# Gate units 5 and 6 of layer 0 as three-pass products, changed orders in layer 0, and blank products at the inner norms

## The reference, cut to what matters

```
z = x @ w_in                        # 1024 -> q 512, k 128, v 128, u 512, two gates of 1024
a = sliding_window_attention(q, k, v, sinks, rel_bias)
s = s5_mixer(u, ...)                # complex diagonal scan, gelu, y * sigmoid(y @ w_glu + b)
merged = sigmoid(g_attn) * (a @ w_branch_attn) + sigmoid(g_ssm) * (s @ w_branch_ssm)
x = layer_norm(ALPHA * x + merged @ w_out)
ffn = swiglu(x) in layer 0, top-2-of-8 experts in layer 1
ple = sigmoid(x @ w_gate) * (p @ w_proj)
x = layer_norm(ALPHA * x + ffn + ple)
```

## Time and profile before

| | us |
|---|---|
| median of three timed runs | 1611.16 |
| the profiled execution's own time | 1609.16 |
| its span in the profile | 1607.3 |
| PE busy | 1570.6 |
| VectorE busy | 1354.6 |
| ScalarE busy | 999.9 |
| PE waiting for VectorE at the norms' transposes (line 1048) | 6.2 + 1.3 |
| PE waiting for the load of a unit of w_in | 2.4 |
| PE waiting for ScalarE before turn_values | 2.1 |

### The profile page before, as it was taken

The page is one execution under the profiler, slowest core; times in us unless marked ns, Lnnn a source line. Parts: engine busy times, 40 slices in busy tenths (PEclk is TensorE's granted clock), DMA queues, the critical chain, the costliest instruction groups (busy, mean ns, idle before and its releaser), DMA issues.

```text
span 1607.3 us, 24068 instructions
## 1 busy us (share of the span) xinstructions
PE 1570.6 (98%) x9028; PEld 1332.7 (83%) x9028; DVE 1354.6 (84%) x1300; ACT 999.9 (62%) x913; POOL 149.8 (9%) x157
## 2 busy tenths in 40 slices
PE   8999999999999999999999999999999999999996
PEld 6889799999899978888888888888888888888884
DVE  8797856655687788999998999998999998999998
ACT  7345444334546437776777777777677677767763
POOL 2000139940300000000000000000000000000000
PEclk9999999999999999999999999999999999999998
DMA  7535855554444568999999999999999999999993
GB/s 225 162 107 183 301 180 192 185 183 132 130 132 148 200 230 297 360 372 359 361 369 334 351 369 370 352 366 334 351 371 360 354 377 332 345 377 364 360 361 124
DMA packets 169448, 456.55 MB, mean 284 GB/s; under 512 B 7638, under 2 KB 60919, under 8 KB 168872
## 3 DMA queue, kind: packets, MB, share of 16 engines
q1 hardware_dynamic: 168472, 450.87, 78.1%
q0 software_dynamic: 768, 4.75, 0.8%
q10 hardware_dynamic: 144, 0.05, 0.0%
HBM read 453.02 MB, written 2.62 MB: 283 GB/s over the span
## 4 chain that ended last, share of the span: by engine, by line
PE 86%; DVE 8%; issue 3%; DMA 1%; ACT 1%; SPq 0%; DVEq 0%; ACTq 0%
PE psum L735 20%; PE psum L737 20%; PE psum L736 20%; PE psum L742 6%; PE psum L744 6%; PE psum L743 6%; PE psum L845 4%; DVE wl L466 2%; PE psum L1199 1%; PE psum L871 1%; ACT wh L460 1%; PE psum L802 1%; DMA ring<-in_w_pg 1%; DVE hid L2190 1%; DMA ring<-in_w_in 1%
## 5 line engine op out<-in xcount | busy, mean ns | idle before, releaser
L466 DVE TENSOR_TENSOR wl<-ring,wh 128x2048 fp32r<-128x2048 f32 x269 | 609.3, 2287 | 67.0 <-ACT wh L460 63.2
L460 ACT ACTIVATE wh<-ring 128x2048 fp32r<-128x2048 f32 x307 | 581.7, 1920 | 126.3 <-PE psum L737 78.4
L736 PE MATMUL psum<-wl,xgh 128*128 128x512 f32 x896 | 349.2, 390 | 0.0
L735 PE MATMUL psum<-wh,xgh 128*128 128x512 f32 x704 | 282.0, 401 | 1.0 <-DVE xgl L2174 0.5
L737 PE MATMUL psum<-wh,xgl 128*128 128x512 f32 x704 | 274.9, 390 | 0.0
L736 PEld LDWEIGHTS psum<-wl,xgh 128*128 128x128 f32 x896 | 168.5, 188 | 32.4
L735 PE MATMUL psum<-wh,hidh 128*128 128x512 f32 x440 | 172.7, 393 | 3.7 <-DVE wl L466 2.8
L736 PE MATMUL psum<-wl,hidh 128*128 128x512 f32 x448 | 174.4, 389 | 0.0
L737 PE MATMUL psum<-wh,hidl 128*128 128x512 f32 x440 | 171.4, 390 | 0.0
L466 DVE TENSOR_TENSOR wl<-ring,wh_spare 128x2048 fp32r<-128x2048 f32 x72 | 164.5, 2284 | 3.0 <-ACT wh_spare L460 3.0
L735 PEld LDWEIGHTS psum<-wh,xgh 128*128 128x128 f32 x704 | 132.2, 188 | 33.6 <-DVE wl L466 5.5
(11 more groups left out here) (435 smaller groups left out, 2769.5 us busy)
## 6 DMA issues: line engine op xcount, KB each, us to landing
ring<-in_moe_gu SPq DMA_DIRECT2D x224, 1024.0 KB, 7.2
ring<-in_moe_dn SPq DMA_DIRECT2D x112, 1024.0 KB, 7.3
ring<-in_w_in SPq DMA_DIRECT2D x25, 1024.0 KB, 5.4
ring<-in_w_gu SPq DMA_DIRECT2D x22, 1024.0 KB, 5.1
ring<-in_w_dn SPq DMA_DIRECT2D x11, 1024.0 KB, 4.9
ring<-in_w_out SPq DMA_DIRECT2D x8, 1024.0 KB, 6.2
ring<-in_w_pg SPq DMA_DIRECT2D x8, 1024.0 KB, 5.2
ring<-in_w_ba SPq DMA_DIRECT2D x4, 1024.0 KB, 5.1
```

The lines of the kernel that those rows point to most:

```text
L460: eng.activation(parts(u)[0], ring[:, ring_slot(u), :], ACT.Copy).then_inc(hi_ready, 1)
L466: eng.tensor_tensor(lo, ring[:, ring_slot(u), :], hi.bitcast(F32), ALU.subtract).then_inc(lo_ready, 1)
L735: pe.matmul(dst, ah, bh, start=first, stop=False, skip_group_check=True)
L736: pe.matmul(dst, ah, bl, start=False, stop=False, skip_group_check=True)
```

## The change

Five things.
1. PLAIN names the plain units of layer 0: 0 to 4, 7 and 8. Units 5 and 6 become split, with high parts in ring slots 4 and 5, and `split_index` counts accordingly. ScalarE writes x0h after the copy of unit 2's q, then the high part of unit 5; that of unit 6 follows copy_maps. VectorE makes both remainders between xIl and scan_states(0).
2. SP issues the load of the state maps of layer 0 (`raw`) after the load of unit 1 instead of before it.
3. local_products(0) stands before turn_values on PE, and ScalarE copies v before k (in both layers).
4. In layer 0 unit 15's high part, and the remainders of 14 and 15, move to the places that they have in layer 1.
5. `turn` begins with `stay_awake`: after `var_ready` of the block PE does AWAKE = 3 plain products of 256 columns with constants into the bank that it turns the block into next. Their results are overwritten.

```
--- before.py
+++ after.py
@@ -42,8 +42,8 @@
 FSTEPS = DFF // 256
 ESTEPS = DFE // 512
 MIXER_UNITS = 22
-FIRST_SPLIT = 9
-PLAIN_UNITS = FIRST_SPLIT
+PLAIN = (0, 1, 2, 3, 4, 7, 8)
+PLAIN_UNITS = len(PLAIN)
 MIXER_RING = 4
 RING_ORDER = (2, 3, 0, 5, 1, 4)
 FREED_BY = {22: 18, 23: 19, 24: 20, 25: 20, 26: 21, 27: 21}
@@ -59,9 +59,11 @@
 LATE_HI = {12: "ring4", 13: "ring5", 14: "late", 15: "ring4", 16: "ring5", 17: "norm", 18: "ring4", 19: "late", 20: "ring5", 21: "ring4"}
 EARLY_HI = {i: ("ring4", "ring5", "early")[i % 3] for i in range(11)} | {11: "turns"}
 ROUNDS = ((0, range(8)), (1, range(4)), (1, range(4, 8)))
-HI_PLACE = ({i: p for i, p in (EARLY_HI | LATE_HI).items() if i >= FIRST_SPLIT}, EARLY_HI | LATE_HI)
+GATE_HI = {5: "ring4", 6: "ring5", 9: "ring4", 10: "ring5", 11: "turns"}
+HI_PLACE = (GATE_HI | LATE_HI, EARLY_HI | LATE_HI)
 EARLY = 4
 WARM = 6
+AWAKE = 3
 GELU_C = 0.7978845608028654
 BIAS_W = 3 * P
 
@@ -394,11 +396,11 @@
 
         def is_split(l, i):
 
-            return l == 1 or i >= FIRST_SPLIT
+            return l == 1 or i not in PLAIN
 
         def split_index(u):
 
-            return u - PLAIN_UNITS
+            return u - sum(p < u for p in PLAIN) if isinstance(u, int) else u - PLAIN_UNITS
 
         def split_used(eng, u, laps=0):
 
@@ -649,10 +651,10 @@
                         load(u, src, ring_slot(u))
                     u += 1
                     if u == 1:
-                        sp.dma_start(raw.rearrange("p a b c -> p (a b c)"), bc_in[0]).then_inc(raw_dma, 16)
                         sp.dma_start(relb_sb[0:BUCKETS + 1], relb).then_inc(table_dma, 16)
                         sp.dma_start(hot_sb[0:BUCKETS + 1], hot_in).then_inc(table_dma, 16)
                     if u == 2:
+                        sp.dma_start(raw.rearrange("p a b c -> p (a b c)"), bc_in[0]).then_inc(raw_dma, 16)
                         small_loads()
                     if u == RING:
                         skew_bias()
@@ -940,7 +942,7 @@
                     project("q")
                     turn_maps(0)
                     project("kv")
-                    turn_values(), local_products(0), input_states(0), scores(0)
+                    local_products(0), turn_values(), input_states(0), scores(0)
                     project("g")
                     input_states(1)
                 else:
@@ -1039,8 +1041,15 @@
                     mm.then_inc(unit_used, 1)
                 u += 4
 
+                def stay_awake(n, b, times):
+
+                    pe.wait_ge(var_ready, NB * n + b + 1)
+                    for _ in range(times):
+                        pe.matmul(bank[OUT_BANKS[2 * b]][:, 0:SEQ], ident, cst[:, 0:SEQ], start=True, stop=True)
+
                 def turn(src, b):
 
+                    stay_awake(1 if src is xa else 2 * l, b, AWAKE)
                     pe.wait_ge(ln_ready, b + 1 + (NB if src is xa else 2 * NB * l))
                     for q in range(2):
                         ps = bank[OUT_BANKS[2 * b + q]]
@@ -1389,15 +1398,18 @@
                     act.activation(qT[:, 2 * (g - 2):2 * (g - 1), :], src, ACT.Copy, scale=HD ** -0.5).then_inc(qk_ready, 1)
                     act.wait_ge(qk_ready, 4 * l + g - 1)
                     act.nop().then_inc(g_free[g % 2], 1)
-                    early_hi(3 + g)
+                    if l:
+                        early_hi(3 + g)
+                    elif g == 2:
+                        act.activation(x0h[:], xT[:], ACT.Copy).then_inc(x0_hi, 1)
+                        early_hi(5)
                 if l == 0:
-                    copy_maps(0)
-                    act.activation(x0h[:], xT[:], ACT.Copy).then_inc(x0_hi, 1)
+                    copy_maps(0), early_hi(6)
+                act.activation(vt.rearrange("p a b -> p (a b)"), group(4)[:, 1, :], ACT.Copy).then_inc(v_ready, 1)
                 for kv in range(2):
                     for q in (0, HD):
                         ins = act.activation(kT[q:q + HD, kv, :], group(4)[kv * HD:(kv + 1) * HD, 0, :], ACT.Copy)
                 ins.then_inc(qk_ready, 1)
-                act.activation(vt.rearrange("p a b -> p (a b)"), group(4)[:, 1, :], ACT.Copy).then_inc(v_ready, 1)
                 act.wait_ge(qk_ready, 4 * l + 3)
                 act.wait_ge(v_ready, l + 1)
                 act.nop().then_inc(g_free[0], 1)
@@ -1439,13 +1451,10 @@
                     if m % 2:
                         act.wait_ge(glu_th, 4 * l + m + 1)
                         act.nop().then_inc(g_free[g % 2], 1)
-                if l == 1:
-                    early_hi(15)
+                early_hi(15)
                 for b in range(2):
                     act.wait_ge(s_ready, 2 * l + b + 1)
                     act.activation(gsh[:, 2 * b:2 * b + 2, :], sT[:, 2 * b:2 * b + 2, :], ACT.Copy, scale=0.25).then_inc(s_hi, 1)
-                if l == 0:
-                    early_hi(15)
                 gates(), copy_probs(2), early_hi(16), copy_attended(2), early_hi(17)
                 for k in range(KD):
                     act.wait_ge(m_ready, KD * l + k + 1)
@@ -2002,6 +2011,7 @@
                     output_powers(dve, link, 0, (scratch_a[:, 0:512], scratch_b[:, 0:512]), 8, (0,))
                     dve.wait_ge(x0_hi, 1)
                     dve.tensor_tensor(xIl[:], xT[:], x0h[:].bitcast(F32), ALU.subtract).then_inc(x0_lo, 1)
+                    early_lo(5), early_lo(6)
                     scan_states(0), logits(0)
                     normalise(0), scan_states(1)
                     output_powers(dve, link, 0, temps, 8, (8,))
@@ -2014,14 +2024,9 @@
                 gelu_half(1), early_lo(12)
                 dve.wait_ge(gelu_ready, 2 * (l + 1))
                 gelu_lo(0), gelu_lo(1), attended_lo(1), logits(2), early_lo(13), normalise(2)
-                if l == 1:
-                    early_lo(14), gated(0), gated(1), early_lo(15)
-                else:
-                    gated(0), gated(1), early_lo(14)
+                early_lo(14), gated(0), gated(1), early_lo(15)
                 dve.wait_ge(s_ready, 2 * (l + 1))
                 gated_lo(0), gated_lo(1)
-                if l == 0:
-                    early_lo(15)
                 attended_lo(2), early_lo(16)
 
 
```

## The result

| us | before | after |
|---|---|---|
| median of five runs each | 1610.77 (1608.92 to 1612.85) | 1603.73 (1603.16 to 1604.67) |
| the profiled execution | 1609.16 | 1603.33 |
| its span | 1607.3 | 1601.5 |
| its mean granted clock | 0.995 | 0.997 |

The ratio of the medians is 0.9948, 95% interval [0.9934, 0.9961]: the change makes the kernel 7.0 us faster. The forecast was 1605.0, with a range of 1602.4 to 1608.2. Between the two profiled executions the difference is 5.8 us, where the sum said 6.1. So the sum nearly holds for the execution that was read, and the medians hold something more; where that is from became the main question of the experiments.

The account below looks back on a forecast made before the run. PE, busy for 98% of the span, was taken to set the pace. Savings of 1.5 + 2.1 + 0 + 0.7 + 1.8 = 6.1 us took 1609.16 to about 1603.0; 2.0 carried over gave 1605.0, range 1602.4 to 1608.2.

Parts of the forecast that it names:

- the sum: Whole kernel: the parts' savings, 1.5 + 2.1 + 0 + 0.7 + 1.8, make 6.1 us.
- The maps' load behind unit 1: Start of layer 0: unit 1 lands sooner, 1.5 us of PE's 2.09 wait saved.
- Local products first: Layer 0, before turn_values: PE's wait of 2.13 us is all removed, 2.1 saved.
- Split units at no cost: Units 5 and 6: ScalarE's and DVE's added work fits idle time; scan_states(0) begins at 60.6 to 60.8.
- Split units without gain: Units 5 and 6: 2.1 us saved on PE is spent waiting at transpose_probs(0); 0 taken.
- first rival: The split units' saving reaches the end: 8.2 us in all, 1603.0; chance 0.13.
- 18.8 us chain: DVE and ACT work from scan_states(0) to the probabilities: same length, starting 3.6 us earlier, ending at 79.65.
- new wait: PE before transpose_probs(0): waits some 1.9 us for DVE's normalise, where it did not wait.
- Units 14 and 15 earlier: Layer 0, before the first branch product: PE's 0.7 us wait for unit 15's remainder goes.
- Blanks: At the norms: clock held, 1.7 us won at the first, 1.1 at the third, 1.0 lost at the second; 1.8 together.
- second rival: At the norms the clock falls despite the blanks: 3.3 us saved in all, 1607.9; chance 0.12.
- The step that failed: End of the sum: the 2.0 us between median and profiled execution is carried over, 1603.0 becoming 1605.0.

Follow-up runs that it names:

- logits first: The changed kernel with logits(0) ahead of scan_states(0) on DVE, so that ScalarE's exponentials run beside the scan: 1602.98 us, ratio 0.9945 to the kernel before.
- values after keys: The changed kernel with turn_values ahead of the local products and ScalarE copying keys before values again: 1607.33 us, ratio 0.9983 to the kernel before.

## Why the prediction was right in its parts, and wrong in its last step

*The maps' load behind unit 1*: 1.5 forecast, 1.75 measured at unit 1.

*Local products first*: 2.1 forecast; the wait of 2.13 is gone and its removal alone is 2.3 at the transposes. Together with the load, less the split units' nothing, 4.08 arrives at transpose_probs(0), where 3.6 to 3.7 was forecast.

*Split units at no cost*: right. The scan begins at 60.41 (60.6 to 60.8 forecast) and ScalarE is ready 1.28 before the value copy.

*Split units without gain*: right, the step on which the forecast differed most from its first rival. The 18.8 us chain did not shrink, the new wait was 2.20 against 1.9, and plain units give the same time at the transposes and at the end. The step rested on two timelines being level (83.26 and 83.44 in the earlier trace rows).

*Units 14 and 15 earlier*: 0.7 forecast; 4.83 - 4.08 = 0.75 measured between the two landmarks. Undoing it cost 1.2 in executions of equal clock (1603.1 to 1601.9), of which 0.7 is the wait; whether the rest is the order's or the w_out load's own scatter is not shown.

*Blanks*: forecast 1.7 + 1.1 - 1.0 = 1.8. From the first norm's transposes to the local products 6.40 - 4.83 = 1.57 was won, at the second norm 1.15 lost, at the third (from the transposes, 5.30 ahead, to the gather, 6.28 ahead) 0.98 won: 1.40. The second rival, a clock that falls all the same, did not happen in the changed kernel, whose five executions all have a mean clock of 0.997. It did happen once with logits first, behind a wait of 2.81 at the third norm. The text gives about 1.4 for each wait at the norms; the third norm's first block had waited 1.98 in the kernel before, and the blanks left 0.58 of it. The Trainium skill, "TensorE: Matmul & The Clock Gate", section "Part 4: PE-mode transpose", says that a transpose does not count as PE being busy in the same way as a product. The runs fit it without proving it: without blanks two waits of 2.52 and 1.45 with only transposes between them were followed by 0.50, and with one blank product ahead of each wait the clock held in the profiled execution.

The terms as measured are 1.75 + 2.33 + 0 + 0.75 + 1.40 = 6.2 (2.33 being what is left of 4.08), and 0.4 to 0.5 of it is lost behind the third norm.

**The step that failed** is the last one of the sum: "The median of the runs is 1611.16, 2.0 above it, and I carry the difference over". The 2.0 are no constant around an execution. They go with the clock: the profiled execution has a mean of 0.995 and two falls, and the median one of the kernel before has 0.993. The experiments show falls behind waits before unit 1 and before turn_values, and without blanks at the norms. The kernel before has these waits, and the change takes them away (and adds one, before the probabilities); after it, the median is 0.4 above the profiled execution and all five have 0.997. That the other executions of the kernel before fell at just these places is inferred from this; no trace of theirs shows it. 1.6 of the error is the 2.0 that became 0.4, and 0.3 in the other direction is the sum of the parts (5.8 measured against 6.1), which gives the 1.27 between 1605.0 and 1603.73. The difference between the medians, 7.0, divides accordingly into some 3 that stay when the clock is equal and some 4 that go with the clock. The parts without the clock had been forecast as 1.5 + 2.1 + 0.7 - 1.0 = 3.3; the clock as 2.8, from the two falls that one execution showed.

The spread of the three runs shown, 2.1 us, against a profiled execution below all of them with a clock of 0.995, could have told it: the text read the clock only where the rows of one execution had it low.

What stays open: which of the places falls how often in the kernel before, and what decides whether a wait is followed by a fall. Each kernel has one profiled execution, and the others give only a mean clock.

## What to carry to other kernels

A wait of PE of about 2 us costs itself and, in some executions, 1.6 us more behind it. So cost a removed or added wait twice: once from the timeline, once from the executions sorted by their mean clock. A new wait that costs nothing by the timeline, since it only replaces work (the 2.20 before the probabilities), is still a place where the clock can fall: of six profiled kernels with it, three lost 1.6 us there.

When an engine is handed work that another did in the critical stretch, follow the longest chain through that stretch before counting the saving. Here one swapped pair of calls (scores' logits ahead of the scan) was needed to free it; after that a load was late next, by an amount that differs from execution to execution.

Put blanks into a wait, and only where the clock is seen to fall. At the norm where PE had worked up to the transposes they cost 1.15 us, and the clock held without them in the profiled executions.

## What the runs showed of the hardware that was not expected

The clock's fall is not fixed by the code. With the same wait before transpose_probs(0), 2.16 to 2.20 us, it held in three kernels (the changed one, no blanks, and blanks only at the first and third norm) and fell to 0.50 at 80 to 82 with units 14 and 15 in the old order, though the code of the four differs only behind this place. Behind a wait of 2.13 or 2.14 before turn_values it held in two kernels (the one before and values after keys), fell for some 4 us in a third and for 13 us in a fourth, with PE busy throughout. The same page of the Trainium skill, section "What's actually happening", says of the first products of a kernel that how many of them run at the lower clock varies from run to run. That is about the start; the rows here show a variation of this kind behind waits in the middle of a kernel.

One fall of the usual length, some 3.4 us at 0.50, costs 1.6 to 1.7 us. With the maps' load first turn_maps come 3.16 late for 1.49 at unit 1, and scores(1) another 1.6 later than that. The longer ones, some 7 us at a norm without blanks and 13 us behind turn_values, cost more.
